# Streaming encoder layer on one core: the next chunk's normalised rows reach the transposed layout by DMA transposes instead of TensorE transposes

## The reference

```python
h = rmsnorm(x, norm_g)
a_b, a_c, a_x, a_g, b_v, b_a, b_g, c_u, c_g, x_q, x_g = split(h @ w_in, 11)   # 256 columns each
y_a = a_b * conv3(a_c * a_x) * silu(a_g)
z   = layernorm(conv31(b_v * sigmoid(b_a)) + bias)
y_b = silu(z) * silu(b_g)
y_c = (per_group_linear(trailing_means_2_4_8_16(c_u) - c_u) + pool_bias) * pool_scale * silu(c_g)
y_x = attention(x_q, 256 memory keys and values, 4 heads) * silu(x_g)
x   = x + concat(y_a, y_b, y_c, y_x) @ w_out
y   = rmsnorm(x, final_norm_g)
```

## Time and profile before

| | us |
|---|---|
| median of three runs | 1609.43 (1607.42 to 1610.38) |
| the profiled execution | 1609.77 |
| its span, first to last instruction | 1607.6 |
| PE busy in it | 1524.6 (95%) |
| DVE busy | 1297.7 (81%) |
| ACT busy | 679.6 (42%) |
| POOL busy | 192.7 (12%) |
| mean granted TensorE clock | 0.981 of full |
| DMA, all from SP's queue | 140.5 MB, 26.5% of 16 engines' span |

### The profile page before, as it was taken

The page is one execution under the profiler, slowest core; times in us unless marked ns, Lnnn a source line. Parts: engine busy times, 40 slices in busy tenths (PEclk is TensorE's granted clock), DMA queues, the critical chain, the costliest instruction groups (busy, mean ns, idle before and its releaser), DMA issues.

```text
span 1607.6 us, 34067 instructions
## 1 busy us (share of the span) xinstructions
PE 1524.6 (95%) x12262; PEld 1323.8 (82%) x12262; DVE 1297.7 (81%) x3323; ACT 679.6 (42%) x1378; POOL 192.7 (12%) x164
## 2 busy tenths in 40 slices
PE   5678999999999999999999999999999999999977
PEld 4567888888888888888888888888888888888865
DVE  6588796969878796978878797978879696988866
ACT  7465334343434335343533435343443435343434
POOL 0011010111111011111111011111110011111100
PEclk9889999999999999999999999999999999999997
DMA  9603303122221303222221402222220312222124
GB/s 284 177 1 128 110 21 124 59 85 78 91 91 56 126 20 100 82 85 78 91 91 31 146 25 85 78 91 91 82 101 20 132 51 85 78 91 86 34 89 120
DMA packets 80867, 140.50 MB, mean 87 GB/s; under 512 B 7113, under 2 KB 32893, under 8 KB 80829
## 3 DMA queue, kind: packets, MB, share of 16 engines
q1 hardware_dynamic: 80829, 140.00, 26.5%
HBM read 122.31 MB, written 17.66 MB: 87 GB/s over the span
## 4 chain that ended last, share of the span: by engine, by line
PE 41%; DVE 33%; issue 18%; ACT 4%; SPq 2%; DMA 1%; DVEq 1%; ACTq 0%
DVE z L1041 13%; PE u L418 7%; PE u L420 7%; PE u L419 7%; PE qps L418 4%; PE qps L420 4%; PE qps L419 4%; PE sps L418 2%; PE sps L419 2%; PE sps L420 2%; DVE pt_lo L1071 2%; DVE probs L1063 2%; ACT probs L758 2%; DVE wo_lo L992 2%; DVE st L1049 1%
## 5 line engine op out<-in xcount | busy, mean ns | idle before, releaser
L418 PE MATMUL u<-h_hi,w_hl 128*128 128x256 f16 (+1 forms) x2992 | 793.7, 271 | 4.1 <-ACT yc L868 2.7
L419 PE MATMUL u<-h_lo,w_hl 128*128 128x256 f16 (+1 forms) x2992 | 792.6, 270 | 0.0
L420 PE MATMUL u<-h_hi,w_hl 128*128 128x256 f16 (+1 forms) x2992 | 792.4, 270 | 0.0
L1041 DVE SCALAR_TENSOR_TENSOR z<-glu,cst,z 128x256 f32<-128x256 f32 (+1 forms) x1020 | 418.7, 477 | 0.5
L418 PEld LDWEIGHTS u<-h_hi,w_hl 128*128 128x128 f16 x2992 | 295.6, 99 | 47.5 <-issue 6.3
L420 PEld LDWEIGHTS u<-h_hi,w_hl 128*128 128x128 f16 x2992 | 295.5, 99 | 33.5
L419 PEld LDWEIGHTS u<-h_lo,w_hl 128*128 128x128 f16 x2992 | 295.7, 99 | 32.3
L701 ACT ACTIVATE gate<-u,inv 128x256 f32<-128x256 f32 (+1 forms) x204 | 83.6, 460 | 224.2 <-PE u L420 224.2
L992 DVE TENSOR_TENSOR wo_lo<-stage,wo_hi 128x512 fp32r<-128x512 f32 x136 | 100.0, 764 | 49.1 <-ACT wo_hi L724 48.8
L418 PE MATMUL sps<-wo_hi,y_hi 128*128 128x512 f32 (+1 forms) x280 | 113.4, 405 | 18.0 <-DVE wo_lo L1083 12.3
L1370 POOL TENSOR_TENSOR sa<-cu 128x540 f32<-128x540 f32 (+1 forms) x17 | 30.7, 1805 | 707.3 <-ACT cu L701 707.3
(11 more groups left out here) (188 smaller groups left out, 2208.4 us busy)
## 6 DMA issues: line engine op xcount, KB each, us to landing
stage<-in_w_out SPq DMA_DIRECT2D x136, 256.0 KB, 5.1
ob<-in_x_prompt SPq DMA_DIRECT2D x34, 512.0 KB, 4.1
probs<-in_w_out SPq DMA_DIRECT2D x68, 256.0 KB, 3.2
out<-ob SPq DMA_DIRECT2D x32, 512.0 KB, 3.1
xb<-in_x_prompt SPq DMA_DIRECT2D x30, 512.0 KB, 4.3
w_hl<-in_w_in SPq DMA_DIRECT2D x20, 512.0 KB, 7.0
sb<-in_w_out SPq DMA_DIRECT2D x34, 256.0 KB, 3.8
sa<-in_w_out SPq DMA_DIRECT2D x34, 256.0 KB, 3.5
```

Source lines behind the costliest of these rows:

```text
L418: nc.tensor.matmul(out, a_hi, b_hi, start=first, stop=False)
L419: nc.tensor.matmul(out, a_hi, b_lo, start=False, stop=False)
L420: return nc.tensor.matmul(out, a_lo, b_hi, start=False, stop=last)
L1041: ins = nc.vector.scalar_tensor_tensor(z[:, c, 0:n], glu[:, c, k:k + n], w, z[:, c, 0:n], ALU.mult, ALU.add)
```

## The change

The rows are split before they are transposed. For the tiles of every chunk but the first, ACT writes the high half of a whole row tile in fp16 in row order (`row_hi`, 128x1024, from `xb`), DVE the low half (`row_lo`), both to a buffer `row16s[t]`, and SP issues a DMA transpose of each half straight to `h_hi` or `h_lo` (`rows_across`): four per chunk, 256 KB each. The buffer of tile 0 is new; that of tile 1 is the memory's norm gain `gm`, which is not used after chunk 0's start. TensorE's 16 transposes per chunk go, with their PSUM slots; the first split b_a waits for the four DMAs (`rows_in`) instead of for `h_lo`. Chunk 0's own rows stay as they were.

Since a row tile is now needed in row order, its whole preparation ends before the chunk's output projection. Tile 0's low half is made right after the second maximum; tile 1 is loaded, squared, scaled and split while the taps run. SP loads tile 1 before the fifth block of w_out (q == 4), and issues the load of the tile after it and the four transposes behind the tenth (q == 9); the wait for `z_back`'s transposes at q == 7, which comes before them in SP's order, is as before.

```diff
+        row16s = [row16, gm[:, :].bitcast(F16).rearrange("p (s d) -> p s d", s=2)]
...
         h_hi_ok, h_lo_ok = signal("h_hi_ok", 4), signal("h_lo_ok", 4)
+        row_hi_ok, row_lo_ok = signal("row_hi_ok", 2), signal("row_lo_ok", 2)
+        rows_in = [signal(f"rows_in{t}", 32) for t in range(2)]
...
-            def sync_chunk(i, n, x_here, y_here, x_next, x_after):
+            def rows_across(rows):
+                for t, m in enumerate(rows):
+                    for half, dst in enumerate((h_hi, h_lo)):
+                        sp.dma_start(dst[:, :, t * P:t * P + m], row16s[t][0:m, half, :],
+                                     transpose=True).then_inc(rows_in[t].sem, 16)
...
+                    if q == 4 and x_next is not None and not (type(i) is int and i == 0):
+                        sp.wait_ge(row_lo_ok.sem, row_lo_ok.at(i, 1))
+                        sp.dma_start(xb[:, :], x_next).then_inc(x_in.sem, 16)
...
-                    if q == 8 and x_next is not None:
-                        v = NFIRST - 2 if type(i) is int and i == 0 else i * len(SLOTS) + NFIRST - 2
-                        sp.wait_ge(u_ready.sem, v)
-                        sp.dma_start(xb[:, :], x_next).then_inc(x_in.sem, 16)
-                if x_after is not None:
-                    sp.wait_ge(u_ready.sem, i * len(SLOTS) + NFIRST)
-                    sp.dma_start(xb[0:x_after.shape[0], :], x_after).then_inc(x_in.sem, 16)
+                    if q == 9 and rows:
+                        sp.wait_ge(row_lo_ok.sem, row_lo_ok.at(i, len(rows)))
+                        if x_after is not None:
+                            sp.dma_start(xb[0:x_after.shape[0], :], x_after).then_inc(x_in.sem, 16)
+                        rows_across(rows)
...
+                    if type(i) is int and i == 0:
+                        pe.wait_ge(h_lo_ok.sem, 4)
+                    else:
+                        for t, _, _ in tiles(n):
+                            pe.wait_ge(rows_in[t].sem, rows_in[t].at(i, 0))
                 for c in range(CT):
...
-                    if nxt and a == 5:
-                        transposes(i, *nxt)
...
                 z_back(i, n)
-                if nxt:
-                    transposes(i, *nxt[0])
                 out_half(i, n, 0)
-                out_half(i, n, 1, nxt[1] if len(nxt) > 1 else None)
+                out_half(i, n, 1)
...
+                    nc.scalar.activation(h_hi[:, 4 * h:4 * h + 4, t * P:(t + 1) * P], src, ACT.Copy).then_inc(h_hi_ok.sem, 1)
+            def row_hi(i, j, t, m):
+                act.wait_ge(x_scaled.sem, j + 1)
+                if needed(rows_in[t].at(i, 0)):
+                    act.wait_ge(rows_in[t].sem, rows_in[t].at(i, 0))
+                nc.scalar.activation(row16s[t][0:m, 0, :], xb[0:m, :], ACT.Copy).then_inc(row_hi_ok.sem, 1)
...
+                if row0:
+                    row_hi(i, *row0)
...
                 nc.scalar.activation(dq_hi[:, :, 0:n], yc[:, :, 0:n], ACT.Copy).then_inc(d_hi.sem, 1)
                 prepare(6)
+                if row1:
+                    squares(row1[0], row1[2], i)
                 scaled_out(i, n, "a_g", gate[:, 2, :, 0:n], ACT.Silu, ag_ok)
...
+                if row1:
+                    row_hi(i, *row1)
...
-                if nxt:
-                    rows_hi(i, nxt[0][0], *nxt[0][1:])
                 y_high(i, n, 2, z[:, :, 0:n], yb_ok)
                 for q in range(WST, PIECES):
                     piece_hi(i, q)
-                    if q == KT + 1 and len(nxt) > 1:
-                        squares(nxt[1][1], nxt[1][3], i)
                     if type(i) is int and i == LAST and q == PIECES - 1:
                         keys_values_hi(1)
-                    if q == KT + 7 and len(nxt) > 1:
-                        rows_hi(i, nxt[1][0], *nxt[1][1:])
                 nt = len(tiles(n))
...
+            def row_lo(i, j, t, m):
+                dve.wait_ge(row_hi_ok.sem, row_hi_ok.at(i, t + 1))
+                nc.vector.tensor_tensor(row16s[t][0:m, 1, :], xb[0:m, :], row16s[t][0:m, 0, :],
+                                        ALU.subtract).then_inc(row_lo_ok.sem, 1)
...
+                if row0:
+                    row_lo(i, *row0)
...
+                if row1:
+                    rows_rms(row1[0], row1[2])
                 taps(i, n, 22, 25)
+                if row1:
+                    rows_scale(row1[0], row1[2])
                 probs_lo(i, n, 1)
                 taps(i, n, 25, TB)
                 prepare(7)
                 prepare(8)
+                if row1:
+                    row_lo(i, *row1)
...
-                if nxt:
-                    rows_lo(i, nxt[0][4], nxt[0][1], 0, nxt[0][2])
                 for q in range(WST, PIECES):
                     piece_lo(i, q)
-                    if q == KT + 2 and len(nxt) > 1:
-                        rows_rms(nxt[1][0], nxt[1][2])
-                    if q == KT + 5 and len(nxt) > 1:
-                        rows_scale(nxt[1][0], nxt[1][2])
                     if q == KT + 3:
```

More of the change, by code:

```diff
@@ L254, in emptied @@
                 name, j = FIRST[n], 0
-                if name[0] == "n":
-                    name, j = "t" + name[1], 1
             else:
                 k = SLOTS.index(name)
[L259 to L264, removed]
+                name, j = (SLOTS[k - 3], i) if k >= 3 else (("x_g", "zb", "c_g")[k], i - 1)
             if name[0] == "t" and name[1:].isdigit():
-                return h_lo_ok.sem, h_lo_ok.at(j, int(name[1]) + 1)
+                return h_lo_ok.sem, int(name[1]) + 1
             s, c = EMPTIED[name]
@@ L397, in prompt_chunk @@
                            x_prompt[0, bass.ds(nxt, P), :] if nxt is not None else None,
-                           x_prompt[0, bass.ds(after, P), :] if after is not None else x_sample[0] if nxt is not None else None)
+                           x_prompt[0, bass.ds(after, P), :] if after is not None else x_sample[0] if nxt is not None else None,
+                           [P, P] if nxt is not None else [SAMPLE])
             prompt_chunk(0, [0, P], N + P, 2 * N)
@@ L420, in three, with transposes @@
                 return nc.tensor.matmul(out, a_lo, b_hi, start=False, stop=last)
-            def transposes(i, names, j, rows=xb):
-                m = j[1]
-                pe.wait_ge(x_scaled.sem, j[0] + 1)
+            def transposes(names, j, rows):
+                i, m = 0, P
+                pe.wait_ge(x_scaled.sem, j + 1)
                 for h, name in enumerate(names):
@@ L545, in z_back, with out_half @@
                 ins.then_inc(u_ready.sem, 1)
-            def out_half(i, n, half, nxt=None):
+            def out_half(i, n, half):
                 banks = sps if half == 0 else qps
@@ L597, in memory_products, with chunk @@
                     ins.then_inc(kvp.sem, 1)
-            def chunk(i, n, nxt):
+            def chunk(i, n):
                 first = type(i) is int and i == 0
@@ L654, in _ @@
             pe.wait_ge(ident_ok.sem, 2)
-            transposes(0, ("t0", "t1"), (0, P), ob[:, 0])
-            transposes(0, ("t2", "t3"), (1, P), ob[:, 1])
+            transposes(("t0", "t1"), 0, ob[:, 0])
+            transposes(("t2", "t3"), 1, ob[:, 1])
             pe.wait_ge(tiny_ok.sem, 1)
@@ L683, in _ @@
             pe.wait_ge(hist_ok.sem, hist_ok.at(CHUNKS, 3))
-            chunk(CHUNKS, SAMPLE, [])
+            chunk(CHUNKS, SAMPLE)
             pe.wait_ge(r_ok.sem, r_ok.at(CHUNKS, 2))
@@ L831, in chunk @@
                 prepare(1)
-                if nxt:
-                    squares(nxt[0][1], nxt[0][3], i)
+                if row0:
+                    squares(row0[0], row0[2], i)
                 scaled_out(i, n, "x_q", dq_hi[:, :, 0:n], ACT.Copy, q_hi)
```

82 lines of the change are left out of this document (40 added, 42 removed).

## The result

The changed kernel takes 1684.87 us (median of four runs, 1681.28 to 1685.71) against 1609.82 us before (four runs): a ratio of 1.047, 95% interval 1.045 to 1.048. The profiled execution has a span of 1683.2 us; before it was 1607.6.

The account below looks back on a forecast made before the run. Each chunk was taken as a ring of two legs, VectorE bounding up to the last tap, then TensorE. 1609.8 + 48.7 (both legs, 3.2 us per loop chunk, plus chunks 0 and 15) + 28 (clock) = 1686 us, range 1650 to 1750.

Parts of the forecast that it names:

- leg 1: From b_v to the last tap, where VectorE sets the time (44.7 us): added work costs 4.0 us, bounds 3.3 to 5.3.
- leg 2: From the z rows through b_a and b_v, where TensorE sets the time (46.5 us): 0.8 us gained, bounds 0.8 to 1.9.
- The wait ahead of the z rows: TensorE, after the second attention product, idles 3.1 us until the last tap, shortly after another 1.6 us idle.
- The clock: TensorE's clock halves around the z rows in two chunks of three, 9.3 times 3.0 us: 28 us, bounds 0 to 51.
- Tile 1's transposes: Eight TensorE transposes removed from each loop chunk, with nothing taking their place: 0.8 us gained.
- Tile 0's transposes: Eight TensorE transposes, about 1 us, removed but valued at nothing: the wait at piece 4 grows by that microsecond.
- DMA transposes in time: Piece 10's block of w_out lands at 8 + T against a deadline of 13.7 us, so the transposes cost nothing.
- T: Time of the four DMA transposes: 3.7 us by bytes, 10.0 by packets; taken as under 5.7, costing nothing.
- the packet price: Each 256-byte row of a transposed block as one packet, 4096 at 39 ns: 10.0 us for the four transposes.
- Clock holds: The 3.1 us wait before the z rows leaves TensorE's clock at full speed: 1658 us, chance 0.22.
- Late transposes: TensorE waits for piece 10 in the output projection's second half: 1751 us, 1901 at twice the packet price; chance 0.28.
- Not slower: TensorE alone bounds, so both tiles' removed transposes save 1.8 us in 15 chunks, 27 us: 1583 us, chance 0.03.

Follow-up runs that it names:

- the run with that work alone: Kernel before the change plus three pieces of unread VectorE work where the change puts its row work, no DMA transposes: 1689.15 us, ratio 1.053.
- The filled gap: Changed kernel without DMA transposes, plus 24 unread matmuls per prompt chunk ahead of TensorE's wait for the last tap: 1655.64 us, against 1677.9 without them.
- the last two runs: Row work behind the taps, SyncE's wait for tile 1's low half moved behind piece 13: 1579.92 us without transfers, 1583.27 with plain copies split between pieces 10 and 14.
- the five profiled kernels with that wait: Changed kernel 1684.9 us; kernel before plus VectorE's work 1689.2; changed without transposes 1677.9; with plain copies 1676.1; without transposes, piece 4's high half earlier, 1669.6.
- the mended order: Row work behind the taps, piece 4's high half earlier, tile 1's low half behind piece 6, chunk 0 as changed: 1602.21 us without transfers, 1702.44 with plain copies.

## Why the prediction was right, step by step

The total came within 2 us of the forecast, closer than its parts: leg 1 was overpriced by 5 us, leg 2's gain by 5 us, and the two cancel. That much is luck.

- **Leg 1, VectorE's work paid in full: right.** 4.0 us said, 3.65 measured (3.7 in the run with that work alone); the terms were 1.13 - 0.34, 1.81 and 1.19 from start to start, 3.79. Working from durations in place of starts overpriced each full-size operation by 0.1 us. The rest is the scaling of tile 0 beside GpSimd, which the prediction left alone: in eight of 14 chunks it took 1.28 us and not 2.13, and the leg was 0.24 us shorter for it.
- **The wait ahead of the z rows, 3.1 us: right**, 3.05 in every chunk of the loop. The one shortly before it, ahead of the second attention product, was 1.2 us and not 1.6.
- **The clock: the sum right, its parts not.** Said: a fall in two of three chunks at 3.0 us each, from the fall in chunk 0. Measured: all 14 chunks, 1.6 us in eleven and 2.9 in three. 28 us said, 27 measured. The two misses cancel, so the 28 is luck; the frequency was a guess and should have been called one. The filled gap shows that the cause was the right one.
- **Tile 1's transposes, 0.8 us: right, and half lost again.** Without transfers leg 2 is 45.6 us where the clock holds, 0.9 less than before. The DMA transposes give 0.46 of it back in the second output half.
- **Tile 0's transposes turned into a wait at piece 4: right.** z back to the first piece shrank from 1.50 to 0.35 us, the first output half grew from 11.52 to 12.64.
- **DMA transposes in time, at cost 0: nearly, by two misses that cancel.** T was to be under 5.7 us. From the first transpose to the issue of piece 10 it was 8.5, and 9.8 to the last landing (735.12 to 742.15, and the median of 2.8 behind it), near the 10.0 us of the packet price that the prediction held too high. By its own sum, 8 + T against 13.7, that is a stall of 2.8 us a chunk. It did not come because the 8 was too long as well: ScalarE had the piece 13.4 us after the load of `sa` (733.25 to 746.66), of which T is 8.5 and all else 4.9. The weak step was to take the blocks ahead at their bytes, 4.6 us; SyncE had issued them and come to the transposes after 1.9. The Trainium skill, in "Advanced Engine Details and Errata" (X-Bar Transpose), has transposing DMAs as fast as plain ones; the landing times in this case agree (2.8 to 7.1 us for a transpose, 4.8 to 8.0 for a plain copy). The 3.7 us that was worked out beside it came from the 284 GB/s and did not hold. The estimate of 42 us, from 1309 ns for a block in the three transpose paths of "VectorE: DVE Perf Modes" in the Trainium skill, is four times the 9.8 us that the rows here give.
- **Rivals.** "Clock holds" (1658) is near what the filled gap made, 1655.6, though that kernel had no transposes either. "Late transposes" (1751 and more) fell; the transposes do cost, but 7 us. "Not slower" fell for the order as written; in the last two runs the same work on VectorE and ScalarE in another order is faster than before, without transfers or with plain copies.

## What to carry to other kernels

When work is added to an engine, first ask on which side of the event that another engine waits for it lands: ahead of the last tap 4 us of VectorE cost 5.5 us a chunk, behind it, once the queue's wait was moved too, the same work cost nothing. An idle gap of the matrix engine is priced twice where it brings the clock down, so a filler or a split gap is worth a run. And every wait in an in-order queue of transfers also delays what stands behind it: moving one wait by four pieces was worth 22 us, and 119 where copies stood behind it (half of them not moved).

## What was unexpected of the hardware

- In the loop the half-speed stretches came in two lengths, 3.4 and 6.8 us, behind equal waits of 3.05 us. In the five profiled kernels with that wait, the clock fell 65 times in chunks 1 to 14. The 19 falls that came 0.74 us or more ahead of the z rows lasted 6.8 us, the 46 later ones (0.67 us ahead to 1.1 behind) 3.4. After 3.05 us of idle the clock fell in 14 of 14 chunks in four profiled kernels and in nine of 14 in one. After 2.3 us at piece 4 it fell in three and in six of 14. After 0.7, 1.3 and 1.5 us ahead of the z rows it never did.
- Where a 128x1024 `scalar_tensor_tensor` of VectorE and an operation of GpSimd start within 0.03 us of each other, one of them is slow: 2.13 us beside 1.08, or 1.28 beside 2.24.
- One of four transfers issued in a row held SyncE far longer than its neighbours, with DMA transposes (1.3, 4.3, 1.3, 1.3 us) and with plain copies at the same place (0.6, 0.7, 4.4, 0.9). In the mended order the copies took 0.6, 0.7, 1.9 and 1.1, and split in two pairs 0.6 and 0.7 each.
- The same four copies cost nothing or 100 us, by what the queue had been waiting for ahead of them.
